# A one-core decoder step: paired attention scores, the first norm's scale and shift on VectorE, merged rows kept on chip

## The chip, the cores and the metric

The kernel runs on one core of a Trainium2 chip. The metric is the device time of one call in microseconds (us), lower is better, as the median of several runs. The core's engines are named as the profile names them: PE is TensorE (PEld its weight loads, PEq its sequencer), DVE is VectorE, ACT is ScalarE, POOL is GpSimd, SP is SyncE.

## What is computed

One layer of a decoder for 1024 prompt tokens and 8 x 8 sample tokens (1088 in all), model width 1024, in float32. Attention comes in three dilation groups over 8 head slots of 64; beside it runs a gated convolution of width 3. What the change touches is, cut from the reference:

```python
# scores of one query block of 128 against its own and the previous key block
scores = jnp.einsum('brnqhc,brnkhc->brnhqk', qb, kk) * (c ** -0.5)
...
br_a = jnp.einsum('nse,ed->nsd', y_att, w_branch_attn)
br_c = jnp.einsum('nse,ed->nsd', c_b * z_conv, w_branch_conv)
merged = jax.nn.sigmoid(g_a) * br_a + jax.nn.sigmoid(g_c) * br_c
mix = jnp.einsum('nsd,de->nse', merged, w_out)
h = layer_norm(DEEPNORM_ALPHA * x + mix, ln1_g, ln1_b)
f = peer_ffn(h, peer_w_q, peer_keys_1, peer_keys_2, peer_u, peer_v)
return layer_norm(DEEPNORM_ALPHA * h + f, ln2_g, ln2_b)
```

`peer_ffn` has 8 retrieval heads. A head scores the token against two lists of 128 keys, takes the 16 best of each, then the 16 best of the pair sums, which name 16 of 16384 experts. Each expert is one row of `peer_u` (a dot product with the token, then GELU) and one row of `peer_v` (weighed by the result and added up).

## The kernel before

**Stages.** The program is a list of phases with all engines meeting between them. The tokens are two halves: EARLY (A) is the first 512 (4 tiles of 128), LATE (B) the other 576 (4 tiles of 128, and one of the 64 sample tokens). In order, with the time at which each runs: `prompt_attn` (0 to 722 us); for A `conv_gates` (732 to 956), `branches` (to 1043) and `mix_ln1` (1045 to 1135); `retrieve_early` (to 1476); for B `conv_gates` (to 1773), `branches` (to 1873), `mix_ln1` (1874 to 2013), `retrieve` (to 2285); `build_gates` (to 2458); `experts` (2461 to 4170); `ln2_out`.

**Split products.** Nearly every product is taken in three parts: each operand is split into a high part of a shorter type (`wh`, `mh`, ACT copies it) and the rest (`wl`, `ml`, DVE or POOL subtracts), and `split3` (lines 79 to 83) issues high x high, high x low, low x high.

**Attention** (`prompt_attn`, line 87). There are 4 slot pairs `s`, each with two heads of 64, which lie in partitions 0 to 63 and 64 to 127 of `qT` and `kT`. A slot pair has 32 units: 16 of kind N (dilation 1; 8 query blocks x 2 heads) and 16 of kind R (the other two groups; 8 tiles x 2 heads). The units of the two heads of one block follow each other. For a unit, PE takes the scores against one or two key blocks per group (`scores`, line 525, into PSUM banks that rotate by three), VectorE adds the mask and takes the maximum, ScalarE takes the exponential, PE transposes the probabilities (`turn_probs`, line 535) and multiplies them with the values (`weigh_values`, line 548). Scores are issued two units ahead; the first two are issued among the last two projection tiles of the slot pair, and ScalarE takes their exponentials among its copies there (`exp`).

**Branches and mixing.** `branches` (line 908) makes the two branch products for each of 8 blocks of 128 output columns, `merge` (line 1002) multiplies them with the gates, adds them, and SyncE stores the block to `s_merged` in DRAM. SyncE loads the branch weights (`r_raw`) block by block, the first one at the start of the phase. `mix_ln1` (line 1103) reads the merged rows back, one tile of 128 tokens at a time (`m_raw`), loads the eight 512 KB blocks of `w_out` over 3 buffers (A) or 2 (B), and multiplies. `Norm` (line 1050) does the first layer norm of each tile: `stats` sums with the residual and takes mean and variance on VectorE, `root` takes the square root on ScalarE, `scale` subtracts the mean and divides on VectorE, and `affine` (lines 1097 and 1099) multiplies with `ln1_g` and adds `ln1_b` on GpSimd, which then stores the row tile to `s_h`. PE transposes the normed tile, and ScalarE and VectorE split it.

**Rows of the experts.** Half A's experts are taken row by row: for each of 512 (token tile, slot) steps GpSimd gathers a 512 KB tile of `peer_u` and one of `peer_v` (`fetch_rows`, lines 605 and 611, over a ring of 4 buffers), and VectorE does `dot_row` (line 623) and `weigh_row` (line 640). `row_step` does one step; there are 528 with the tail. The steps are laid into the phases of half B: `ROWS_IN = (60, 16, 16)` says how many lie in `conv_gates`, `branches` and `mix_ln1` of B, and the rest is in `experts`. Half B's experts are computed in `experts` for all 16384 experts with PE.

**Early retrieval** (`retrieve_early`, line 1282) does 8 retrieval heads for half A and, woven into them, the cached attention of 8 sample batches. One round of its loop takes query and key scores of one head (PE), `mask_scores` of one batch and `rank`, `pairs`, `finish` of earlier heads (VectorE), `choose` (ScalarE) and `look_up` (GpSimd), which find the index of a chosen expert by a one-hot product. SyncE's loop is

```python
for i in range(HEADS):
    if i + 1 < HEADS:
        for x in range(2):
            load_w(i + 1, x)
    load_values(i)            # waits for the value product of batch i - 1
    if i + 1 < DB:
        load_new(i + 1)       # waits for the turn of batch i
        load_keys(i + 1)
```

where `new` (line 1371) are the queries and keys of the sample tokens, which PE turns at line 1689, `KT` the cached keys and `V` (`cache_v`, line 1383) the cached values, 2.3 MB a batch.

## Time and profile before

| | |
|---|---|
| runs of the kernel | 4220.33, 4224.22, 4226.38 us; median 4224.22 |
| the profiled execution | 4224.69 us; span of its profile 4222.9 us |
| PE busy | 3685.5 us (87%) |
| DVE busy | 3001.5 us (71%) |
| ACT busy | 1240.1 us (29%) |
| POOL busy | 1843.2 us (44%) |
| DMA | 1024.51 MB, mean 243 GB/s |

The span is the time from the first to the last instruction that the profiler saw; all times of the trace are from its start. A busy time is the sum over an engine's instructions, so an engine that is at 87% over the whole span can be full in one stage and half idle in another. The slices of the span show that, each digit being tenths:

```profile
PE   8999998997676399776773999999999999999998
...
DVE  4434433333355668668687979999998999999996
...
PEclk9999998998777699988876999999999999999999
DMA  4122121896444278786201889999999999999996
```

### The profile page before, as it was taken

To read this page: it belongs to the slowest core of one execution; us is meant where nothing else is said; L and a number is where in the kernel's file an instruction comes from. 1 tells how busy PE (TensorE), PEld (TensorE's weight loads), DVE (VectorE), ACT (ScalarE), POOL (GpSimd) and SP (SyncE) were. 2 spreads that over 40 slices of the span, in tenths; PEclk is the share of its full clock that TensorE was granted. 3 is DMA by queue.
4 is the path that set the end of the run, shared out by engine and by line. 5 is a ranking of instruction groups with operands and counts; after the bars stand their busy time and mean duration, and the time that the engine had idled before them with its cause. 6 is when DMAs were issued, how large, how long until landed. Compare 5 with 4: busy or idle time off the path is not lost. (4 is left out here: it accounts for less than half of the span.)

```text
span 4222.9 us, 64289 instructions
## 1 busy us (share of the span) xinstructions
PE 3685.5 (87%) x24855; PEld 3441.4 (81%) x24855; DVE 3001.5 (71%) x5899; ACT 1240.1 (29%) x2036; POOL 1843.2 (44%) x1382
## 2 busy tenths in 40 slices
PE   8999998997676399776773999999999999999998
PEld 8899896885555299764762889999999999999996
DVE  4434433333355668668687979999998999999996
ACT  2323313221233322211334952222222222222221
POOL 0000000000334435436576956666666666666661
PEclk9999998998777699988876999999999999999999
DMA  4122121896444278786201889999999999999996
GB/s 144 26 74 68 28 74 31 329 360 200 159 145 162 73 257 311 289 308 208 75 21 34 231 289 368 371 377 375 379 381 357 376 378 378 369 364 377 378 361 220
DMA packets 485059, 1024.51 MB, mean 243 GB/s; under 512 B 50977, under 2 KB 257441, under 8 KB 482841
## 3 DMA queue, kind: packets, MB, share of 16 engines
q0 software_dynamic: 149264, 543.49, 34.5%
q1 hardware_dynamic: 334264, 472.56, 32.5%
q8 instruction: 191, 3.13, 0.3%
q10 hardware_dynamic: 1232, 4.46, 0.3%
q14 instruction: 108, 0.88, 0.1%
HBM read 942.84 MB, written 131.28 MB: 254 GB/s over the span
## 5 line engine op out<-in xcount | busy, mean ns | idle before, releaser
L605 POOL DMA_INDIRECT u_row<-in_peer_u_dram,eid x512 | 731.6, 1429 | 646.0 <-DVE dots L623 556.5
L611 POOL DMA_INDIRECT v_row<-in_peer_v_dram,eid x512 | 583.5, 1140 | 193.4 <-issue 155.8
L640 DVE SCALAR_TENSOR_TENSOR f_row<-v_row,g_coef,f_row 128x1024 f32<-128x1024 f32 x508 | 661.4, 1302 | 1.5 <-DMA v_row<-in_peer_v_dram,eid 1.2
L81 PE MATMUL e_ps<-coef_h,v_h 128*128 128x288 f32 x2048 | 614.4, 300 | 44.9 <-DVE v_l L2318 28.2
L623 DVE CUSTOM_DVE_ANT_0 u_row<-u_row,h_row 128x1024 f32<-128x1024 f32 x512 | 630.9, 1233 | 5.0 <-DMA h_row<-s_h 2.7
L81 PE MATMUL e_ps<-tokens_Bh,u_h 128*128 128x288 f32 x2048 | 608.1, 297 | 7.0 <-DVE u_l L2312 7.0
L83 PE MATMUL e_ps<-coef_h,v_l 128*128 128x288 f32 x2048 | 609.8, 298 | 0.0
L82 PE MATMUL e_ps<-coef_l,v_h 128*128 128x288 f32 x2048 | 609.2, 297 | 0.0
L82 PE MATMUL e_ps<-tokens_Bl,u_h 128*128 128x288 f32 x2048 | 607.4, 297 | 0.0
L83 PE MATMUL e_ps<-tokens_Bh,u_l 128*128 128x288 f32 x2048 | 604.6, 295 | 0.0
L81 PEld LDWEIGHTS e_ps<-coef_h,v_h 128*128 128x128 f32 x2048 | 390.2, 191 | 57.1 <-DVE v_l L2318 36.3
L81 PEld LDWEIGHTS e_ps<-tokens_Bh,u_h 128*128 128x128 f32 x2048 | 386.2, 189 | 7.5 <-DVE u_l L2312 7.5
L82 PEld LDWEIGHTS e_ps<-coef_l,v_h 128*128 128x128 f32 x2048 | 390.2, 191 | 0.0
L83 PEld LDWEIGHTS e_ps<-coef_h,v_l 128*128 128x128 f32 x2048 | 389.8, 190 | 0.0
L83 PEld LDWEIGHTS e_ps<-tokens_Bh,u_l 128*128 128x128 f32 x2048 | 387.1, 189 | 0.0
L82 PEld LDWEIGHTS e_ps<-tokens_Bl,u_h 128*128 128x128 f32 x2048 | 386.4, 189 | 0.0
L276 POOL DMA_DIRECT2D s_att<-attS x4 | 2.3, 584 | 721.7 <-ACT attS L336 721.7
L2271 ACT ACTIVATE v_h<-v_raw 128x512 fp32r<-128x512 f32 x256 | 158.8, 627 | 423.4 <-PE e_ps L83 393.3
L2256 ACT ACTIVATE x_tmp<-e_ps 128x576 f32<-128x576 f32 x128 | 83.3, 651 | 489.2 <-PE e_ps L83 488.4
L81 PE MATMUL c_psB<-tokens_Bh,c_whB 128*128 128x288 f32 x640 | 193.0, 302 | 20.5 <-DVE c_wlB L818 20.5
L82 PE MATMUL c_psB<-tokens_Bl,c_whB 128*128 128x288 f32 x640 | 191.6, 299 | 0.0
L83 PE MATMUL c_psB<-tokens_Bh,c_wlB 128*128 128x288 f32 x640 | 190.8, 298 | 0.0
(425 smaller groups left out, 8538.7 us busy)
## 6 DMA issues: line engine op xcount, KB each, us to landing
u_raw<-in_peer_uT_dram SPq DMA_DIRECT2D x128, 512.0 KB, 7.5
v_raw<-in_peer_vQ_dram SPq DMA_DIRECT2D x256, 256.0 KB, 6.6
s_g<-gate_block SPq DMA_DIRECT2D x9, 4096.0 KB, 16.3
x_gate<-s_g SPq DMA_DIRECT2D x64, 576.0 KB, 7.3
out_o_kv_sample_dram<-in_cache_kv_w_dram SPq DMA_DIRECT2D x32, 1016.0 KB, 8.0
c_rawA<-in_conv_tiles_dram SPq DMA_DIRECT2D x40, 512.0 KB, 5.6
c_rawB<-in_conv_tiles_dram SPq DMA_DIRECT2D x40, 512.0 KB, 6.3
w_raw<-in_w_in_dram SPq DMA_DIRECT2D x96, 192.0 KB, 3.7
```

The costliest lines, as they stand in the source:

```text
L81: pe.matmul(out, lh, rh, start=first, stop=False)
L82: pe.matmul(out, lh, rl, start=False, stop=False)
L83: return pe.matmul(out, ll, rh, start=False, stop=last)
L276: pool.dma_start(io["s_att"][s][:, :SEQ], attS[:]).then_inc(att_out, 16)
L605: pool.indirect_dma_start(k["u_row"][:, r % RING], None, io["peer_u"][0], bass.IndirectOffsetOnAxis(ap=k["eid"][:, r:r + 1], axis=0)).then ...
L611: pool.indirect_dma_start(k["v_row"][:, v % RING], None, io["peer_v"][0], bass.IndirectOffsetOnAxis(ap=k["eid"][:, v:v + 1], axis=0)).then ...
L623: dve.tensor_tensor_reduce(row, row, k["h_row"][:, t % 2], 1.0, 0.0, ALU.mult, ALU.add, k["dots"][:, s % 2, x:x + 1]).then_inc(k["dotted"], 1)
L640: dve.scalar_tensor_tensor(out=f, in0=row, scalar=coef, in1=f, op0=ALU.mult, op1=ALU.add).then_inc(k["weighed"], 1)
L2256: act.activation(tmp[:, e % 2].rearrange("p (y n) -> p y n", y=2), ps[:, 2 * (e % 2):2 * (e % 2) + 2, :CW], ACT.Gelu).then_inc(gelu_done, 1)
L2271: act.activation(vh[:, n % VS], vraw[:, n % VR], ACT.Copy).then_inc(v_hi, 1)
```

## The change

1. **Scores of two heads in one call.** `scores(s, u)` now issues both heads of a block, units `u` and `u + 1`: block by block of 128 keys, first partitions 0 to 63, then 64 to 127, into two PSUM banks. A pair is issued after `turn_probs(s, u)` of every even `u`; the first pair is issued at the last projection tile, and ScalarE takes its two exponentials before the copy of that tile.
2. **Branch weights.** The first block of branch weights is loaded in the middle of `conv_gates`.
3. **Merged rows stay in SBUF** (`merged_A`, `merged_B`, each in two parts), the store to `s_merged` and the loads back are gone, and the splits read the two parts. The eight blocks of `w_out` are loaded during `branches` into a place of their own.
4. **The norm.** `stats` adds a pass (y - mean) x gain on VectorE after the variance; `scale` is (y / std) + bias. `affine` is gone, and GpSimd only stores.
5. **Expert rows.** `ROWS_IN` is (60, 16, 0): the 16 steps of `mix_ln1` are done in `experts`.
6. **Early retrieval.** SyncE loads `new` and the keys of the next batch ahead of the values of this one. ScalarE's `choose` is two functions, `weights` and `one_hot`, issued at the head's start and between the queries; GpSimd's `look_up` is split in the same way into `distances` and `look_up`.

The diff, cut (unchanged in meaning where left out: the placement of the buffers in SBUF):

```diff
-ROWS_IN = (60, 16, 16)
+ROWS_IN = (60, 16, 0)
...
-                        if ri == 2 and t >= PT - 2:
-                            exp(s, t - (PT - 2))
+                        if ri == 2 and t == PT - 1:
+                            exp(s, 0)
+                            exp(s, 1)
...
             def scores(s, u):
-                kind, where, h = units[u]
...
+                kind, where, _ = units[u]
+                for x in (u, u + 1):
+                    if x >= SR:
+                        pe.wait_ge(s_free, s * NU + x - SR + 1)
...
-                off = 0
-                for g in ((0,) if kind == "N" else (1, 2)):
-                    tiles = [j for gg, j in key_blocks(u) if gg == g]
-                    n = len(tiles) * P
-                    m = pe.matmul(ps[:, s_bank(s, u), off:off + n], qT[h * HD:(h + 1) * HD, g, q * P:(q + 1) * P],
-                                  kT[h * HD:(h + 1) * HD, g, tiles[0] * P:tiles[0] * P + n], start=True, stop=True)
-                    off += n
-                m.then_inc(s_ready, 1)
+                blocks = key_blocks(u)
+                for x, (g, j) in enumerate(blocks):
+                    for h in range(2):
+                        rows = slice(h * HD, (h + 1) * HD)
+                        m = pe.matmul(ps[:, s_bank(s, u + h), x * P:(x + 1) * P], qT[rows, g, q * P:(q + 1) * P],
+                                      kT[rows, g, j * P:(j + 1) * P], start=True, stop=True)
+                        if x == len(blocks) - 1:
+                            m.then_inc(s_ready, 1)
...
-                scores(s, 3)
                 for u in range(2, NU):
-                    if u + 2 < NU:
-                        scores(s, u + 2)
...
                     turn_probs(s, u)
+                    if u % 2 == 0 and u + 2 < NU:
+                        scores(s, u + 2)
...
+                if n == NQ // 2:
+                    load_branch(sp, k, io, 0)
...
-                sp.wait_ge(br_done, NC * (j + 1))
-                sp.dma_start(io["s_merged"][j][:, cols], mg[:, j % 2]).then_inc(mg_out[j % 2], 16)
-            for x in range(2):
-                sp.wait_ge(mg_out[x], 16 * KD // 2)
+                sp.dma_start(k["w_out"][half.name][:, j], io["w_out"][0, j * P:(j + 1) * P]).then_inc(k["o_in"][j], 16)
...
         dve.bn_aggr(self.mv[:n, x], self.st[:n, x]).then_inc(self.var_ready, 1)
+        dve.drain()
+        dve.scalar_tensor_tensor(out=y, in0=y, scalar=self.mv[:n, x, 0:1], in1=self.gain[:n], op0=ALU.subtract, op1=ALU.mult)
...
-        dve.tensor_scalar(self.y[:n, x], self.y[:n, x], self.mv[:n, x, 0:1], self.rstd[:n, x:x + 1],
-                          ALU.subtract, ALU.mult).then_inc(self.scaled, 1)
-
-    def affine(self, pool, t, x, n):
-        pool.wait_ge(self.scaled, t + 1)
-        pool.tensor_tensor(self.y[:n, x], self.y[:n, x], self.gain[:n], ALU.mult).then_inc(self.gained, 1)
-        pool.wait_ge(self.gained, t + 1)
-        pool.tensor_tensor(self.y[:n, x], self.y[:n, x], self.bias[:n], ALU.add).then_inc(self.ready, 1)
-
+        dve.scalar_tensor_tensor(out=self.y[:n, x], in0=self.y[:n, x], scalar=self.rstd[:n, x:x + 1], in1=self.bias[:n],
+                                 op0=ALU.mult, op1=ALU.add).then_inc(self.ready, 1)
...
-    at_row = spread(y0, rows, [1] * (TL - 1) + [0])
+    at_row = spread(y0, rows, [1] * TL)
...
-                act.activation(mh[:, x, :, :n], raw[:, x, :, :n], ACT.Copy).then_inc(m_hi, 1)
+                for part in range(2):
+                    m = act.activation(mh[:, x, part * KD // 2:(part + 1) * KD // 2, :n], merged(i, part), ACT.Copy)
+                m.then_inc(m_hi, 1)
...
-                load_values(i)
                 if i + 1 < DB:
                     load_new(i + 1)
                     load_keys(i + 1)
+                load_values(i)
...
+                if i >= 2:
+                    weights(i - 2)
+                    one_hot(i - 2, 0)
                 if i < HEADS:
                     query(i, 0)
                     split_w(i + 1, 0)
                 if i >= 1:
                     copy_probs(i - 1)
+                if i >= 2:
+                    one_hot(i - 2, 1)
...
-                if i >= 2:
-                    choose(i - 2)
...
             for i in range(HEADS + 1):
-                if i < HEADS:
-                    for x in range(2):
+                if i >= 2:
+                    distances(i - 2)
+                for x in range(2):
+                    if i < HEADS:
                         query(i, x)
                         split_w(i + 1, x)
-                if i >= 2:
-                    look_up(i - 2)
+                    if i >= 2:
+                        look_up(i - 2, x)
```

PE in prompt attention, where the first slot pair goes over into its units of kind N, before (`a_ps` is PSUM, `S` the probabilities, `PTs` their transposes, `vR` the values; x2 is two such instructions in a row):

```order
L525 MATMUL a_ps<-kT,qT 128x256 x2
L535 MATMUL a_ps<-ident,S 128x128 x2
L548 MATMUL a_ps<-vR,PTs 128x64
L525 MATMUL a_ps<-kT,qT 128x256
L535 MATMUL a_ps<-ident,S 128x128 x2
L548 MATMUL a_ps<-vR,PTs 128x64 x2
```

and the same place in the changed kernel:

```order
L528 MATMUL a_ps<-kT,qT 128x128 x4
L551 MATMUL a_ps<-vR,PTs 128x64
L538 MATMUL a_ps<-ident,S 128x128 x2
L551 MATMUL a_ps<-vR,PTs 128x64 x2
L538 MATMUL a_ps<-ident,S 128x128 x2
L528 MATMUL a_ps<-kT,qT 128x128 x4
```

A score product of 256 columns for one head stood ahead of each unit; now four products of 128 columns, two for each head, stand ahead of every second one, between the transposes and the values of a unit.

SP in the early retrieval, one round, before (`q_rawA` are the query weights of the next head):

```order
L1382 DMA new<-s_qkv 24x1x512
L1383 DMA cache_v<-in_cache_vS_dram 128x4608
L1371 DMA new<-s_qkv 24x1x512 x2
L1376 DMA KT<-in_cache_kT_dram 128x4x128
L1377 DMA KT<-in_cache_kT_dram 128x4x1024
L1365 DMA q_rawA<-in_peer_w_q_dram 128x8x128 x2
```

and in the changed kernel:

```order
L1365 DMA q_rawA<-in_peer_w_q_dram 128x8x128 x2
L1371 DMA new<-s_qkv 24x1x512 x2
L1376 DMA KT<-in_cache_kT_dram 128x4x128
L1377 DMA KT<-in_cache_kT_dram 128x4x1024
L1382 DMA new<-s_qkv 24x1x512
L1383 DMA cache_v<-in_cache_vS_dram 128x4608
```

`new` x2 and the two loads of `KT` now stand ahead of the batch's value loads (L1382, L1383) and not behind them.

DVE in `mix_ln1` of half A, one tile, before:

```order
L1076 SCALAR_TENSOR_TENSOR n1A_y<-n1A_res,m_psA 128x1024
L1080 BN_STATS n1A_st<-n1A_y 128x6 x2
L1082 BN_AGGR n1A_mv<-n1A_st 128x2
L1090 RECIPROCAL n1A_rstd<-n1A_std 128x1
L1092 TENSOR_SCALAR n1A_y<-n1A_y,n1A_mv,n1A_rstd 128x1024
```

and in the changed kernel:

```order
L1084 SCALAR_TENSOR_TENSOR n1A_y<-n1A_res,m_psA 128x1024
L1088 BN_STATS n1A_st<-n1A_y 128x6 x2
L1090 BN_AGGR n1A_mv<-n1A_st 128x2
L1092 SCALAR_TENSOR_TENSOR n1A_y<-n1A_y,n1A_mv,n_affineA 128x1024
L1100 RECIPROCAL n1A_rstd<-n1A_std 128x1
L1102 SCALAR_TENSOR_TENSOR n1A_y<-n1A_y,n1A_rstd,n_affineA 128x1024
```

The pass with the gain stands between the variance and the root's result, and the last pass adds the bias.

## Rows read from the trace of the kernel before

**Rows 1.** Windows: stretch, length, busy us of each engine, PEclk, DMA share, GB/s.

```profile
0.00:732.00 732.00, 699.50 (x4232) 641.02 (x4232) 290.81 (x795) 211.95 (x576) 2.54 (x8) 0.99 0.22 62
...
300.00:370.00 70.00, 69.76 (x438) 57.50 (x437) 30.98 (x118) 35.99 (x110) 0.00 (x0) 1.00 0.13 28
...
1140.00:1476.00 336.00, 201.76 (x1754) 161.00 (x1754) 185.80 (x956) 109.76 (x194) 146.46 (x80) 0.73 0.41 142
...
1886.00:2016.00 130.00, 76.52 (x282) 54.69 (x282) 93.00 (x101) 23.53 (x28) 72.66 (x48) 0.75 0.62 209
...
2460.00:4173.00 1713.00, 1660.37 (x12288) 1647.74 (x12288) 1578.72 (x2100) 451.10 (x694) 1094.13 (x848) 0.99 0.97 365
```

**Rows 2.** Timeline of TensorE in attention: start, us, line, operation, shapes, [idle before].

```profile
318.81 0.70 PE L525 MATMUL a_ps<-kT,qT 64*128 64x256 f32 x2
319.44 0.44 PE L535 MATMUL a_ps<-ident,S 128*128 128x128 f32 x2
...
320.20 0.70 PE L525 MATMUL a_ps<-kT,qT 64*128 64x256 f32 x2
...
328.52 0.71 PE L525 MATMUL a_ps<-kT,qT 64*128 64x128 f32 x4
```

**Rows 3.** Timeline of TensorE in the early retrieval: transposes, and 32-column strips.

```profile
1213.56 1.14 PE L1713 MATMUL q_psA<-ident,Ss 128*128 128x128 f32 x9
...
1222.75 2.17 PE L1725 MATMUL q_psA<-cache_v,PTss 128*32 128x128 f32 x72
```

**Rows 4.** Timeline of ScalarE: the first branch weights, early and late.

```profile
968.66 1.48 ACT L985 ACTIVATE r_whA<-r_rawA 128x1536 fp32r<-128x1536 f32 x1 [12.86 <-DMA r_rawA<-in_w_branch_conv_dram]
...
1778.17 1.48 ACT L985 ACTIVATE r_whB<-r_rawB 128x1536 fp32r<-128x1536 f32 x1 [11.43 <-DMA r_rawB<-in_w_branch_conv_dram]
```

**Rows 5.** Timeline of the mixing stages, early, then late (from 1874.52).

```profile
1041.79 0.69 DVE L1012 TENSOR_TENSOR r_mgA<-r_mgA,r_tcA 128x512 f32<-128x512 f32 x1
...
1053.14 0.77 PE L81 MATMUL m_psA<-o_whA,m_hA 128*128 128x512 f32 x1 [12.85 <-DVE o_wlA L1213]
...
1081.02 1.22 DVE L1076 SCALAR_TENSOR_TENSOR n1A_y<-n1A_res,m_psA 128x1024 f32<-128x1024 f32 x1 [7.58 <-PE m_psA L83]
...
1108.71 1.21 DVE L1076 SCALAR_TENSOR_TENSOR n1A_y<-n1A_res,m_psA 128x1024 f32<-128x1024 f32 x1
...
1121.36 1.21 DVE L1076 SCALAR_TENSOR_TENSOR n1A_y<-n1A_res,m_psA 128x1024 f32<-128x1024 f32 x1
...
1125.73 2.33 POOL L1097 TENSOR_TENSOR n1A_y<-n1A_y,n1A_gain 128x1024 f32<-128x1024 f32 x1 [6.88 <-DVE n1A_y L1092]
...
1874.52 0.06 DVE L1072 MEMSET n1B_eps<- 128x1 f32 x1 [0.42 <-PEq L912]
...
1920.06 1.22 DVE L1076 SCALAR_TENSOR_TENSOR n1B_y<-n1B_res,m_psB 128x1024 f32<-128x1024 f32 x1 [8.15 <-PE m_psB L83]
...
1925.42 3.41 DVE L640 SCALAR_TENSOR_TENSOR f_row<-v_row,g_coef,f_row 128x1024 f32<-128x1024 f32 x1
...
1940.42 1.21 DVE L1076 SCALAR_TENSOR_TENSOR n1B_y<-n1B_res,m_psB 128x1024 f32<-128x1024 f32 x1
```

**Rows 6.** Waits, 1135 to 1476: engine, line, waited for: us, times, longest.

```profile
PE q_psA L1689 <- DMA new<-s_qkv: 72.1, 7, 12.4
```

**Rows 7.** Timeline of VectorE in the early retrieval, one head.

```profile
1179.37 1.38 DVE L1633 CUSTOM_DVE_ANT_0 Ss<-q_psA,smask 128x1176 f32<-128x1176 f32 x1 [7.28 <-PE q_psA L1702]
...
1217.15 1.38 DVE L1633 CUSTOM_DVE_ANT_0 Ss<-q_psA,smask 128x1176 f32<-128x1176 f32 x1 [7.82 <-PE q_psA L1702]
...
1224.24 3.75 DVE L1583 TENSOR_TENSOR candA<-top_vA 128x256 f32<-128x256 f32 x2
...
1237.02 0.23 DVE L1604 TENSOR_TENSOR pos_parts_fA<-best_pos_fA,row_firstA 128x64 f32<-128x64 f32 x1
...
1255.96 0.68 DVE L1618 TENSOR_REDUCE selA<-q_hotA 128x64 f32<-128x512 f32 x1 [9.08 <-issue]
```

**Rows 8.** Windows: a stretch in the middle of the expert stage.

```profile
3300.00:3500.00 200.00, 197.67 (x1485) 196.80 (x1485) 190.04 (x253) 54.52 (x83) 134.66 (x105) 1.00 0.99 379
```

170 lines of the change are left out of this document (91 added, 79 removed).

## The prediction

> **What bounds the kernel now.** I read the busy time by stage first. The reader is to see five different limits [rows 1]. In prompt attention (0 to 732 us) TensorE is busy 699.5 of 732. In the early retrieval (1140 to 1476) it is busy 201.8 of 336 at a mean granted clock of 0.73, with the DMA engines at 0.41, so something waits there. In the late mixing stage (1886 to 2016) it is busy 76.5 of 130. In the expert stage (2460 to 4173) TensorE is at 1660 of 1713, VectorE at 1579 and the DMA engines at 0.97: three resources are nearly full. The stages follow each other behind barriers, so a gain in one is a gain at the end, if a later stage isn't given more work. This change does both.
>
> **Paired scores.** Attention handles 32 units for each of 4 slot pairs. A unit's score product of 256 columns is two passes that hold TensorE 0.63 us (318.81 to 319.44) of a unit of 1.39 us (to 320.20) [rows 2]. A unit with two products of 128 columns takes four passes in 0.71. One pair has 14 units of the first kind, 2 of half that, 8 with four short passes, and 8 with two 256-column products: 14 x 0.63 + 2 x 0.32 + 8 x 0.64 + 8 x 1.26 = 24.7 us, 98.6 for all four. The change issues the same columns as passes of 128, alternating between partitions 0 to 63 and 64 to 127. If the two halves of the array work at once, this halves: -49 us. No row shows two row halves at work together. The nearest shows four column strips: 72 passes of 128 columns in 2.17 us, 0.03 each, against 1.14 for 9 passes across the whole array, 0.13 each [rows 3]. So work in separate parts of the array does overlap here, by four. What is late next: ScalarE is busy 36.0 us over 32 units, 1.12 each (300 to 370 us) [rows 1], and TensorE would need 1.39 - 0.31 = 1.08 for a two-block unit. ScalarE, or the chain score, mask, exponential, transpose, which now has less work of TensorE to hide under, takes some back in the first 16 units. I give it 4 us: **-45**. The ends: 0 (no overlap; the columns are the same) and -55 (switching between array shapes half as often).
>
> The Trainium skill (TensorEngine Tiling, Tiling Modes and Theoretical Speedup) says that two tiles of 64 rows run in parallel, up to 2 times as fast. By it alone this term is -49; no row here shows it for row tiles.
>
> **Weights of the branches loaded ahead.** ScalarE waited 12.9 us (early) and 11.4 (late) for the first branch weights [rows 4]; 8.1 and 4.7 of it lie behind the stage's start, since loads were only issued there. They now land during the convolution stage. The attention rows that the branches also need still load at the start, so I take 6 early; late, where 4 MB of output weights come into a stage that also gathers expert rows, 2.5. **-8.5**. The ends: 0 and -13. The 0.8 MB added to each convolution stage I put at **+1** together.
>
> **Merged rows kept on chip, output weights loaded ahead.** Early: the first output matmul starts at 1053.14, 10.7 us after the last merge, and the first tile is summed at 1081.02 [rows 5]. Between them TensorE waits for eight 512 KB weight loads over two or three buffers. Now nothing is stored and read back, and all eight lie in SBUF. What remains ahead of the first matmul is two splits (some 1.3 us each on ScalarE and VectorE) and the first weight split, another pass of 1.2: some 4.3 us with the starts. The eight splits go at VectorE's 1.23 us, so the first half tile takes 10.4, about its pace at the low clock, and the second 24 matmuls x 0.23 = 5.6: 16 us for 28. That is -6.4 - 11.4 = -17.8. Late: the sum at 1920.06 is 45.5 us after the stage's start at 1874.52 [rows 5]; in its place stand 4.1 and 16.4: -25.
>
> **The norm and the sixteen rows.** GpSimd's two passes stood between VectorE and the transposes: 2.33 each early, 4.7 and a start together, and not less late [rows 5]. VectorE now does (y - mean) x gain in one pass of about 1.25 beside ScalarE's root, and one more in place of the scale. The wait behind a tile falls by 3.5 to 4 us. It counts at the last tile of each half, with 0.6 to 1 at the one before. Between them tiles are paced by TensorE at 12.65 us (1108.71 to 1121.36), where VectorE needs some 8 us. -5 early, -4 late. Late, tiles take 20.4 us (1920.06 to 1940.42), because four row steps of VectorE lie in each and are caught by GpSimd: a weighing step that ends beside it takes 3.41 us. With 16 rows gone and GpSimd quiet they should take the early 12.7 to 13: 4 x -7.2 = -29. Sum of this and the part before: -22.8 early, -58 late, **-81**. Ends: -60, -92.
>
> **Early retrieval.** TensorE waits 72.1 us in seven waits for `new` [rows 6]. SyncE issues it only after `load_values`, which waits for the previous batch's value product; and its 0.1 MB then stand in the queue behind 2.3 MB of values. The change issues `new` and the keys a whole head earlier, so the wait should go. What is late next is VectorE: mask, one rank and the pairs run without a gap from 1217.15 to 1237.25 (20.1 us); the other rank takes what this one did, 5.7 from the mask's end to 1224.24, and the two parts of `finish` some 2.2 [rows 7]. That is 28.0 us a head, with starts 28.2, where a head took 37.8 (mask to mask, 1179.37 to 1217.15) and TensorE's busy time is 201.8 over 8 heads. `finish` waited 9.08 us for the look-up [rows 7]. Moving the one-hot work to the start of a head on ScalarE and GpSimd puts it beside mask, rank and pairs, and I cost the moved instructions at nothing under that cover of some 20 us; uncovered they would be 10 to 15 a head. Seven heads x 9.5: **-66**. Ends: -45, -72.
>
> **Experts.** The 16 rows come here. Each is two gathers of 512 KB, in all 16.8 MB, and 16 x 2.5 us of VectorE, which would be busy 1619. The stretch 3300 to 3500 shows the DMA engines at 0.99 with 379 GB/s [rows 8]. At this rate 16.8 MB are 44 us of all engines. There is slack of some 10 to 15 us in the middle of the stage (shares of 0.98 to 0.99) and none that these rows can reach at its ends. **+35**. Ends: +5 and +50.
>
> The Trainium skill (DMA: Bandwidth & Descriptors, Where 436 GB/s comes from) puts the ceiling at 435 GB/s. By it 379 is not full, the rows would fit, and the sum below would be 30 us lower. The same page's HBM limit of 358 is already exceeded by the row.
>
> **The sum:** -45 - 8.5 + 1 - 81 - 66 + 35 = -164.5. The profiled execution took 4224.69 us (span 4222.9); that gives 4060. It is 0.5 above the median, so the forecast is **4060** against 4224.22. A difference of 0.2% (8.4 us) is about what a measurement can tell.
>
> **Rivals.**
> - *The halves don't overlap.* Two row halves write the same PSUM partitions, which column strips do not. Attention then gains nothing: 4060 + 45 = 4105. The strips speak against it. 8%.
> - *The expert stage takes the rows for nothing.* For: VectorE waits for gathered rows almost nowhere, GpSimd waits for VectorE. Against: the share of 0.99. Then 4060 - 30 = 4030. 10%.
> - *The retrieval finds another wait.* In SyncE's new order the value load of one batch stands ahead of the next head's query weights; if these come late, or ScalarE, which now waits for VectorE at the head's start, delays the next query's copy, a head takes 32 and not 28: -40 for -66, so 4086. 12%.
> - *The change doesn't do what it says:* the loads ahead land late and the mixing stages keep half of their waits: 4060 + 25 = 4085. 4%.
> - *Slower: starved experts lose the clock.* The granted clock is 1.00 in the stretch shown and 0.73 where TensorE waits [rows 1, 8]. A 288-column matmul comes every 0.135 us (1485 in 200) and would come every 0.27 at the low level. If gathers delay weights so that TensorE idles often, 1270 of 12288 matmuls at the low level give back 172 us, the 164 and 0.2%. That is a mean clock of 0.95 for 0.99 in the stage. The stage would have to be starved ten times as much as its present loss. Time from 4233 on. 2%.
>
> **How the numbers follow.** My forecast has 64%, its own range 4040 to 4085. To hold 8 in 10 I add the case of no overlap and that of free rows, and leave out the far ends: **4028 to 4100**. Faster than before by over 0.2% is all but the last rival and a little for what I don't see: 0.97; within 0.2% 0.01; slower 0.02.
>
> **What would show it.** In the profile after: attention ends near 675 instead of 722, with score pairs of 0.6 to 0.7 us (1.26 if the halves don't overlap). The wait of TensorE for `new` is gone, and a head lasts 27 to 29 us. No wait for output weights in the mixing stages, tiles of 12.5 to 13 us in both. The expert stage lasts some 1748 us with the DMA engines at 0.98 or more, TensorE's busy share down to about 0.95 and new waits for `v_raw` and `u_raw` or for gathered rows. If the stage still lasts 1713, my reading of the DMA share is wrong; if a head still takes over 32, my reading of the retrieval is.

## The result, and the profile after

The changed kernel takes 4022.68 us (median of 4 runs, 4021.18 to 4025.86) against 4222.62 for the kernel before in the same comparison: a ratio of 0.9527, 95% interval 0.9510 to 0.9543. The forecast was 4060 with a range of 4028 to 4100, so the sign was right and the time lay 5 us below the range. The profiled execution took 4025.86 us, with a span of 4024.1 for 4222.9 before: -198.8 where the sum said -164.5. Among all the executions behind this document one stands apart: of the four of run e11 one took 12239.65 us at a granted clock of 0.41, the others 4012 to 4016; e11's median below counts it, its ratio doesn't.

Each stage's length below is read in the two timelines, from the first instruction of a phase to the first of the next one, with the forecast's term beside it.

| stage | before | after | change | forecast |
|---|---|---|---|---|
| attention | 727.0 | 691.0 | -36.0 | -45 |
| convolution, early | 232.5 | 231.8 | -0.7 | +0.5 |
| branches, early | 84.8 | 78.3 | -6.5 | -6 |
| mixing, early | 90.1 | 66.9 | -23.2 | -22.8 |
| early retrieval | 341.2 | 259.1 | -82.1 | -66 |
| convolution, late | 297.1 | 297.1 | 0.0 | +0.5 |
| branches, late | 101.1 | 95.8 | -5.3 | -2.5 |
| mixing, late | 138.6 | 77.5 | -61.1 | -58 |
| retrieval, late | 273.2 | 268.0 | -5.2 | 0 |
| gates of the experts | 172.6 | 172.6 | 0.0 | 0 |
| experts | 1711.5 | 1733.0 | +21.5 | +35 |
| last norm | 52.5 | 52.3 | -0.2 | 0 |

The windows of the changed kernel, with the columns of [rows 1], show the same five stages:

```profile
0.00:692.00 692.00, 659.15 (x4472) 621.84 (x4472) 285.40 (x795) 206.53 (x576) 2.55 (x8) 0.99 0.23 64
...
1069.00:1328.00 259.00, 188.11 (x1754) 147.26 (x1754) 194.85 (x960) 111.27 (x194) 147.46 (x81) 0.82 0.54 187
...
1720.00:1798.00 78.00, 63.39 (x280) 48.72 (x280) 47.04 (x60) 19.93 (x29) 4.68 (x8) 0.89 0.28 100
1798.00:2066.00 268.00, 146.19 (x1010) 142.85 (x1010) 208.25 (x1109) 94.63 (x155) 172.47 (x97) 0.76 0.11 32
...
2239.00:3972.00 1733.00, 1668.86 (x12288) 1658.10 (x12288) 1615.98 (x2150) 451.11 (x697) 1132.13 (x880) 0.98 0.98 370
```

In the early retrieval TensorE has the same 1754 matmuls in 259 us and not 336, at a granted clock of 0.82 for 0.73. In the late mixing stage GpSimd is busy 4.7 us where it was busy 72.7. The expert stage moves 370 GB/s for 365 at a DMA share of 0.98 for 0.97. The late retrieval, in which nothing was changed, gained 5.2 us; its granted clock is 0.76 (0.74 before), and TensorE's busy time there is 6.3 us shorter for the same matmuls.

**Attention.** TensorE's timeline of the changed kernel, in the first units of a slot pair:

```profile
302.67 0.71 PE L528 MATMUL a_ps<-kT,qT 64*128 64x128 f32 x8
303.32 0.43 PE L551 MATMUL a_ps<-vR,PTs 128*128 128x64 f32 x2
...
304.92 0.71 PE L528 MATMUL a_ps<-kT,qT 64*128 64x128 f32 x8
...
307.64 0.44 PE L538 MATMUL a_ps<-ident,S 128*128 128x128 f32 x2 [0.81 <-ACT S L317]
308.01 0.71 PE L528 MATMUL a_ps<-kT,qT 64*128 64x128 f32 x8
```

Eight passes of 128 columns hold TensorE 0.65 us (302.67 to 303.32), where four took 0.64 [rows 2]. So the two halves of the array do work at once. Sixteen passes (a pair with two key blocks in each of two groups) hold it 1.09 us, where eight passes of 256 columns for the same two units took 2 x 1.06 before. The grouped lines say it for the whole stage, before (two groups) and after:

```profile
L525 PE MATMUL a_ps<-kT,qT 64*128 64x256 f32 x240 | 72.3, 414 | 0.0
...
L525 PE MATMUL a_ps<-kT,qT 64*128 64x128 f32 x144 | 26.6, 300 | 0.0
```

```profile
L528 PE MATMUL a_ps<-kT,qT 64*128 64x128 f32 x624 | 52.0, 293 | 0.0
```

The scores take 52.0 us for 98.9, a gain of 46.9, and the stage gained 36.0. The other 11 are given back at several places. Most pairs of eight passes follow each other by 2.24 us where two units took 2 x 1.39 = 2.78, so 0.54 of the 0.61 is kept. One of the first pairs takes 3.09 (304.92 to 308.01), with a wait of 0.81 for ScalarE's exponential; nine such waits in the stage add up to 4.7 us. And the first pair of sixteen passes is followed by the next one after 3.38 us, where its two units took 2 x 1.82 before.

**Early retrieval.** No wait for `new` is left among TensorE's waits. VectorE's timeline, two heads in a row:

```profile
1161.78 1.38 DVE L1643 CUSTOM_DVE_ANT_0 Ss<-q_psA,smask 128x1176 f32<-128x1176 f32 x1 [0.23 <-PE q_psA L1712]
...
1168.87 3.79 DVE L1593 TENSOR_TENSOR candA<-top_vA 128x256 f32<-128x256 f32 x2
1172.58 2.38 DVE L1597 CAST top_ifA<-top_iA 128x128 f32<-128x128 uint32 x1
...
1189.97 1.38 DVE L1643 CUSTOM_DVE_ANT_0 Ss<-q_psA,smask 128x1176 f32<-128x1176 f32 x1
...
1197.41 0.69 DVE L1593 TENSOR_TENSOR candA<-top_vA 128x256 f32<-128x256 f32 x2
1198.02 0.22 DVE L1597 CAST top_ifA<-top_iA 128x128 f32<-128x128 uint32 x1
```

The first of these two heads lasts 28.19 us, the forecast's 28.2 to the tenth. But the pair sums and the cast, 6.2 us in it, take 0.9 in the next head. That one lasts 25.4 and not 23, since two of its later passes are slow in their place (1.42 and 1.19 us, for 0.23 and 0.26 in the first). What stands beside the slow pair sums and cast is in GpSimd's timeline:

```profile
1168.66 1.28 POOL L1527 TENSOR_TENSOR q_lA<-q_fullA,q_hA 128x512 fp32r<-128x512 f32 x1
1169.90 2.54 POOL L1523 TENSOR_TENSOR q_wlA<-q_rawA,q_whA 128x1024 fp32r<-128x1024 f32 x1
1172.40 2.48 POOL L1540 TENSOR_TENSOR q_hotA<-q_hotA,top_ifA 128x1024 f32<-128x1024 f32 x1
```

VectorE's passes end at 1172.66 and 1174.96; GpSimd's end at 1172.44 and 1174.88. Each VectorE pass is done 0.1 to 0.2 us after a GpSimd pass ends. The seven heads, from mask to mask, take 22.5, 23.9, 25.0, 28.2, 25.4, 28.4 and 26.1 us, 25.6 on average. Before they took 24.4, 37.8, 46.0, 38.6, 36.8, 38.7 and 37.6, 37.1 on average. The 46.0 is the head from 1217.15 to 1263.14 [rows 7]:

```profile
1246.11 0.22 DVE L1609 TENSOR_REDUCE totA<-exA 128x4 f32<-128x64 f32 x1 [8.86 <-ACT exA L1434]
...
1263.14 1.38 DVE L1633 CUSTOM_DVE_ANT_0 Ss<-q_psA,smask 128x1176 f32<-128x1176 f32 x1
```

The first two heads have less to do than the others: in the loop the pair sums start with the second head and `finish` with the third.

**Mixing.** The first output product and the first two tile sums of the late stage, which starts at 1720.76:

```profile
1724.46 0.77 PE L81 MATMUL m_psB<-o_whB,m_hB 128*128 128x512 f32 x1 [10.23 <-DVE o_wlB L1213]
...
1738.96 1.22 DVE L1084 SCALAR_TENSOR_TENSOR n1B_y<-n1B_res,m_psB 128x1024 f32<-128x1024 f32 x1 [5.49 <-issue]
...
1753.12 1.21 DVE L1084 SCALAR_TENSOR_TENSOR n1B_y<-n1B_res,m_psB 128x1024 f32<-128x1024 f32 x1
1756.09 1.28 DVE L1092 SCALAR_TENSOR_TENSOR n1B_y<-n1B_y,n1B_mv,n_affineB 128x1024 f32<-128x1024 f32 x1
1757.52 1.28 DVE L1102 SCALAR_TENSOR_TENSOR n1B_y<-n1B_y,n1B_rstd,n_affineB 128x1024 f32<-128x1024 f32 x1
...
1765.09 1.21 DVE L1084 SCALAR_TENSOR_TENSOR n1B_y<-n1B_res,m_psB 128x1024 f32<-128x1024 f32 x1
```

The first product comes 3.7 us after the start (forecast 4.1), the first sum 18.2 after it (forecast 20.5; 45.5 in [rows 5]). The first two sums are 14.2 us apart, the others 12.0 (forecast 12.5 to 13) for 20.4.

### The profile page after: what moved, and what is told of

Same layout as the page of the kernel before. It is cut to its first block and busy times, and to the rows that moved or that the text cites. A ratio compares the mean times of both kernels' runs of the same rounds, so it can differ in the third digit from the quotient of the medians.

```text
span 4024.1 us, 64681 instructions
## 1 busy us (share of the span) xinstructions
PE 3616.4 (90%) x25095; PEld 3404.7 (85%) x25095; DVE 2998.9 (75%) x5917; ACT 1229.7 (31%) x2041; POOL 1790.2 (44%) x1364
## 5 line engine op out<-in xcount | busy, mean ns | idle before, releaser
L642 DVE SCALAR_TENSOR_TENSOR f_row<-v_row,g_coef,f_row 128x1024 f32<-128x1024 f32 x508 | 652.7, 1285 | 3.9 <-DMA v_row<-in_peer_v_dram,eid 2.8
L625 DVE CUSTOM_DVE_ANT_0 u_row<-u_row,h_row 128x1024 f32<-128x1024 f32 x512 | 621.8, 1215 | 5.1 <-DMA h_row<-s_h 2.8
L2266 ACT ACTIVATE x_tmp<-e_ps 128x576 f32<-128x576 f32 x128 | 83.2, 650 | 419.7 <-PE e_ps L83 400.7
L81 PE MATMUL c_psB<-tokens_Bh,c_whB 128*128 128x288 f32 x640 | 192.6, 301 | 20.5 <-DVE c_wlB L834 20.5
## 6 DMA issues: line engine op xcount, KB each, us to landing
s_g<-gate_block SPq DMA_DIRECT2D x9, 4096.0 KB, 16.1
```

What stands on the lines that cost most here:

```text
L81: pe.matmul(out, lh, rh, start=first, stop=False)
L625: dve.tensor_tensor_reduce(row, row, k["h_row"][:, t % 2], 1.0, 0.0, ALU.mult, ALU.add, k["dots"][:, s % 2, x:x + 1]).then_inc(k["dotted"], 1)
L642: dve.scalar_tensor_tensor(out=f, in0=row, scalar=coef, in1=f, op0=ALU.mult, op1=ALU.add).then_inc(k["weighed"], 1)
L2266: act.activation(tmp[:, e % 2].rearrange("p (y n) -> p y n", y=2), ps[:, 2 * (e % 2):2 * (e % 2) + 2, :CW], ACT.Gelu).then_inc(gelu_done, 1)
```

## The experiments

All are the changed kernel with one edit, unless said otherwise. "The call" is the median; ratios are to the kernel before, run in the same comparison. The early retrieval, where it wasn't edited, lasted from 249.8 to 259.1 us over twelve profiles (mean 254.3), so 5 us in that stage of one profile tell nothing; the changed kernel's own profile has the longest of them, and by the other eleven this stage gained more than 82 us. Attention, where it wasn't edited, lasted 688.5 to 691.0, the early branch stage 75.2 to 79.0, the late one 95.1 to 97.0. The interval of a ratio is about 7 us to either side. Stages are read in one profile a run, with the marks of the table above; the expectations of e1 to e4 take attention, the early retrieval and late mixing by other marks (680.9, 256.6 and 81 us where the table has 691.0, 259.1 and 77.5).

### Do the halves of the array need to alternate? (e1, e7)

```diff
-                for x, (g, j) in enumerate(blocks):
-                    for h in range(2):
+                for h in range(2):
+                    for x, (g, j) in enumerate(blocks):
```

> The changed kernel, with the four (or eight) passes of a score pair issued head by head: all passes of partitions 0 to 63 first, then all of 64 to 127. Same passes, same place. In the changed kernel attention lasts 680.9 us (716.7 before) and eight passes of 128 columns take 0.71 us. If it is the alternation that lets the two halves of the array work at once, eight passes take some 1.1 to 1.3 us again and attention some 700 to 725 us, the call some 4045 to 4065. If TensorE overlaps the halves in whatever order they come, or if the gain is that a pair switches the array's shape half as often, attention stays at 681 and the call at 4023.

4023.31 us, 0.9525 (0.9509 to 0.9540), the same as the changed kernel within the interval. But attention lasted 696.6 us, outside the 688.5 to 691.0 of the others, and the rows say why. The pairs of eight passes hold TensorE 0.65 us as before, those of sixteen 1.64 and not 1.09. Here is e1, then the changed kernel, then one unit of the two before:

```profile
303.60 0.72 PE L528 MATMUL a_ps<-kT,qT 64*128 64x128 f32 x8
...
167.82 1.71 PE L528 MATMUL a_ps<-kT,qT 64*128 64x128 f32 x16
```

```profile
168.05 1.16 PE L528 MATMUL a_ps<-kT,qT 64*128 64x128 f32 x16
```

```profile
347.88 1.13 PE L525 MATMUL a_ps<-kT,qT 64*128 64x256 f32 x4
```

All four such pairs of every slot pair are like this, 16 x 0.55 = 8.8 us, and the scores take 61.1 us in all for 52.0. So with four passes of one half in a row the order doesn't matter; with eight in a row about half of the overlap is lost (2 x 1.06 = 2.12 without any, 347.88 to 348.94 being one unit). Why it is lost there is not shown. The first rival of the expectation is thus right for the long pairs and wrong for the short ones.

> The changed kernel, with the scores of a pair issued as before the change in passes of up to 256 columns, the one head's behind the other's. If it is enough that work of both halves of the array stands next to each other in TensorE's queue, attention stays at 691 us (679 to 695) and the call at 4023, perhaps a little less since half as many passes and weight loads are issued. If the short passes matter for the overlap, score pairs of two key blocks take some 1.26 us and not 0.65, and attention lasts 715 or more.

The edit puts the old loop over groups of up to 256 columns inside a loop over the two heads. 4019.19 us, 0.9516 (0.9500 to 0.9531); attention 689.2 us. A pair of two key blocks is four passes in 0.63 us, and the long pair is eight passes, four for each head in a row, in 1.07. So short passes aren't needed, and it is the number of passes in a row that cost e1 its overlap, not their columns, which are the same here. Whether this is faster than the changed kernel isn't shown (the intervals overlap).

### What the two new orders of the early retrieval are worth (e2, e3, e6)

```diff
+                load_values(i)
                 if i + 1 < DB:
                     load_new(i + 1)
                     load_keys(i + 1)
-                load_values(i)
```

> The changed kernel, with SyncE's old order in the early retrieval: the values of a batch ahead of the next batch's new rows and keys. The stage lasts 256.6 us in the changed kernel, 338.6 before. If the wait for the new rows was what set the pace, the stage comes back to 320 to 338 us and the call to 4085 to 4105, with TensorE waiting some 60 to 72 us for new rows. If the moved one-hot work was as much of it, the stage stays below 310.

4093.73 us, 0.9691 (0.9675 to 0.9707): 71 us given back. The stage lasts 329.0 us, its heads behind the first 37.4 to 37.7, and the wait is there again among TensorE's waits:

```profile
PE q_psA L1699 <- DMA new<-s_qkv: 69.2, 7, 11.5
```

> The changed kernel, with the look-up of ScalarE and GpSimd back at the end of a head, and SyncE's new order kept. If the look-up only hides under VectorE, the stage stays within 5 us of 256.6. If VectorE's last step of a head waits for it once the new rows are early, the 9 us wait is there again and the stage lasts some 290 to 320 us (10 to 15 us a head uncovered, part of it under what SyncE gained), the call 4055 to 4085.

The edit puts `weights` and both `one_hot` calls behind `keep(i - 1)`, and `distances` and both `look_up` calls behind the loop over `x`, as they stood before. 4046.16 us, 0.9581 (0.9565 to 0.9597): 23 us. The stage lasts 280.4, less than expected, its third head 36.1 and the later ones 29.8 to 30.4. So SyncE's order alone brings 341.2 to 280.4 (-60.8), the look-up's place alone 341.2 to 329.0 (-12.2), and both together -82 to -91. Of the 12.2 the third head has 8.5 (46.0 to 37.5): in it VectorE has its slow passes beside GpSimd and then waits 8.86 us for ScalarE and 9.08 for the look-up [rows 7], and the next mask stands right behind. In the four heads after it the look-up's place brings 0.4 us each while TensorE waits for `new`, and some 3 once it doesn't.

```diff
                 dve.tensor_tensor_reduce(S[:], flat[:, S0:S0 + W], mask[:], SCALE, LOW, ALU.add, ALU.max, mx[:])
                 dve.drain()
+                dve.tensor_tensor_reduce(S[:], flat[:, S0:S0 + W], mask[:], SCALE, LOW, ALU.add, ALU.max, mx[:])
+                dve.drain()
```

> The changed kernel, with VectorE's mask pass of the early retrieval (1.38 us, once a batch) issued twice, which gives the same result and 1.5 us more of VectorE in each of 8 heads. The stage lasts 259 us. If VectorE sets the pace of the heads now, +10 to 12 us. If TensorE's own products or ScalarE's copies do, 0 to 4 us.

4035.01 us, 0.9545 (0.9530 to 0.9561): 12.3 more, and 270.0 us in the stage, 15.7 above its mean. Eight passes of 1.5 are 12. VectorE sets the pace of the heads behind the first.

### What a VectorE pass waits for beside GpSimd (e11, e18)

In e11 GpSimd's passes of 1024 elements in the early retrieval are two of 512, one after the other; here the look-up's, the other two likewise:

```diff
-                pool.tensor_tensor(hot[:, x], hot[:, x], ixf[:, h % 2, x].unsqueeze(2).to_broadcast([P, TL, K, K]),
-                                   ALU.mult)
+                for a in (slice(0, TL // 2), slice(TL // 2, TL)):
+                    pool.tensor_tensor(hot[:, x, a], hot[:, x, a],
+                                       ixf[:, h % 2, x, a].unsqueeze(2).to_broadcast([P, TL // 2, K, K]), ALU.mult)
```

> The changed kernel, with GpSimd's passes of 2.4 us in the early retrieval (weight splits, distances, look-up) issued as two halves each. Heads there take 23.9 to 28.8 us, and in the long ones VectorE's pair sums take 3.8 us and not 0.8. If such a pass of VectorE waits until GpSimd's running pass ends, its slow passes shrink to 1.2 to 1.5 us, and the stage falls by 5 to 12 us below 253 to 259. If the two share a path at a lower rate, or VectorE waits until GpSimd has nothing left, the pair sums stay at 3.8 in the heads that meet GpSimd and the stage is the same within 3 us.

4014.32 us (4012.57 over the other three), 0.9499 (0.9480 to 0.9518), an interval that overlaps the changed kernel's. The stage lasted 247.2 us, its heads after the first two 25.1 to 25.8 where they had been 25 or 28. VectorE's cast beside GpSimd's passes of this kernel:

```profile
1190.57 1.30 DVE L1602 CAST top_ifA<-top_iA 128x128 f32<-128x128 uint32 x1
```

```profile
1188.96 1.48 POOL L1529 TENSOR_TENSOR q_lA<-q_fullA,q_hA 128x512 fp32r<-128x512 f32 x1
1190.39 2.61 POOL L1524 TENSOR_TENSOR q_wlA<-q_rawA,q_whA 128x512 fp32r<-128x512 f32 x2
```

The cast ends at 1191.87, not with the pair of GpSimd's passes (1193.0) but about where its first half ends (1190.39 + 2.61 / 2 = 1191.7). A slow cast is 1.3 us now and was 2.4, a slow pair sum 1.4 and was 2.5: VectorE's pass waits until the running pass of GpSimd ends. The Trainium skill says so (SBUF — State Buffer, Who interferes with whom): the two engines have one port pair in common, which a GpSimd instruction that reads SBUF holds to its end, while a VectorE instruction with two SBUF inputs, or a copy or cast in a two-port mode, waits. These rows agree for the pair sums and the cast. With e15 and e16, which have the same halves (251.1 and 248.0 us), the stage is 248.8 us on average of three profiles, for 254.3.

> The changed kernel, with GpSimd's passes of 2.4 us in the early retrieval in quarters. With halves VectorE's slow passes fell from 2.5 to 1.4 us and the call to 4014.3 (0.9499 of before). If VectorE waits for the end of the running pass, they fall to 0.8 to 1.0, and the stage by 2 to 4 us more, unless what a further start costs GpSimd makes the look-up late: then the stage grows by 3 or more, and VectorE waits for it again.

4017.24 us, 0.9514 (0.9495 to 0.9532), the stage 252.7: no further gain, against the expected 2 to 4 us. Some slow passes did fall to 0.75 us, but the longest stayed at 1.3 to 1.5, since GpSimd's passes of 1.3 us (the query's split, the look-up's fold) were not cut. GpSimd's weight splits now take 45.4 us in all and not 38.5.

### The late mixing stage (e9, e10, e12, e4, e13)

e9 restores `tensor_scalar` in `scale`, `affine` on GpSimd and its two semaphores, and takes the pass with the gain out of `stats`.

> The changed kernel, with the norm's scale and shift back on GpSimd (two passes of 2.33 us a tile behind VectorE), no expert rows in the mixing stages. The mixing stages last 66.9 (early) and 77.5 us (late). If the passes only count at the end of a half and a little before, as forecast, +5 early and +4 late, the call +9. If GpSimd's passes slow VectorE's splits and sums in every tile, +2 or more a tile, the call +18 or more. If they are hidden, 0.

4028.78 us, 0.9531 (0.9515 to 0.9547). The stages last 72.2 (+5.3) and 83.9 (+6.4), where 5 and 4 were forecast. 3.4 us of each lie behind the last sum (13.7 and 12.6 us to the stage's end, for 10.3 and 9.2), the other 1.9 and 3.0 between the sums.

e10 takes the load of `w_out` out of the loop of `branches`, and in `mix_ln1` it reads

```diff
+            for j in range(KD):
+                sp.dma_start(k["w_out"][half.name][:, j], io["w_out"][0, j * P:(j + 1) * P]).then_inc(k["o_in"][j], 16)
             N.load(sp)
```

> The changed kernel, with the eight loads of the output weights at the start of the mixing stage in place of the branch stage, into the same eight buffers, the merged rows kept on chip. 4 MB take 11 to 12 us, and the first product waits for the first block and the norm's loads. Mixing stages +8 to +12 each (the rest of the 23 and 61 us came from the buffers, the norm and the rows), branch stages -1 to -5 each since they load 4 MB less. If the early loads are hidden in the branch stage for nothing, those stay at 78 and 96.

4030.67 us, 0.9535 (0.9519 to 0.9551). Mixing 72.2 (+5.3) and 85.7 (+8.2); branches 75.2 (-3.1) and 95.1 (-0.7), no shorter than in other runs that keep the loads there. So the early loads cost the branch stages nothing that these profiles can tell, and the early mixing stage gave back less than the 8 expected.

> The changed kernel, with the 16 expert rows back in the late mixing stage, spread over its five tiles. The expert stage lasts 1732.7 us in the changed kernel and 1711.2 before. It should come back to 1711, which gives the price of 16 rows there, 21 us and not the 35 forecast. In the mixing stage (81 us now) the rows cost 16 x 2.5 = 40 us of VectorE in tiles of 12.7 us where VectorE needs 8: if GpSimd's two passes were what made them dear, +20 to 25 us and the call the same as the changed kernel within 5 us; if the rows themselves are dear beside the norm, +30 to 40 and the call 10 to 20 us slower.

4028.35 us, 0.9533 (0.9518 to 0.9549), with `ROWS_IN = (60, 16, 16)`. Experts 1711.1 (-21.9), mixing 93.7 (+16.2). The 16 rows cost there less than the 20 to 25 expected. But the late retrieval lasted 285.3 (+17.3). TensorE's waits in it name a small table:

```profile
PE q_psB L2021 <- DMA count16B<-in_c_count_dram: 15.7, 1, 15.7
```

> The changed kernel, with 16 expert rows back in the late mixing stage, over its first four tiles only. With five tiles the late retrieval lasted 285.3 us for 268.0, and TensorE waited 15.8 us for its small count table. If that wait came from the gathers issued behind the last tile, the retrieval is back at 268, the mixing stage stays at 94 to 98 and the expert stage at 1711, and the call takes 4016 to 4021. If not, the retrieval stays at 285 and the call at 4028.

Beside `ROWS_IN`, e12 has

```diff
-    at_row = spread(y0, rows, [1] * TL)
+    at_row = spread(y0, rows, [1] * (TL - 1) + [0])
```

4026.46 us, 0.9529 (0.9513 to 0.9545). The table's wait is 5.0 us as in the changed kernel; the retrieval lasts 276.2, mixing 95.8 (+18.3), experts 1710.7. So the gathers behind the last tile caused the long wait, though the retrieval didn't come all the way back to 268. e4's profile is of the slowest of its four executions (4034.61), and the medians of e4 and e12 are 1.9 us apart: whether the others had the long wait isn't shown. Rows in the mixing stage are no better than rows with the experts.

The late retrieval's length differs with the number of row steps done ahead of it, but neither grows nor falls with it: 273.2 to 276.2 us with 92 (the kernel before, e8, e12, e13), 266.2 to 268.3 with 76 (the changed kernel and every one with its rows), 271.5 with 60 (e5). In e8 none of the 92 lay in the mixing stage, so gathers still under way are not the reason. What is stays open.

e13 is e9 and e12 together.

> The changed kernel, with both the norm's scale and shift back on GpSimd and 16 expert rows in the first four tiles of the late mixing stage. Alone the first cost that stage 6.4 us (83.9 for 77.5) and the second 18.3 (95.8). If they add up, the stage lasts 102. If rows and GpSimd's passes lengthen each other, as the kernel before suggests with tiles of 20.4 us, it lasts 110 to 125, and a weighing step beside GpSimd takes 3.4 us again.

4044.96 us, 0.9573 (0.9557 to 0.9589). The late mixing stage lasts 111.8 us, 34.3 more than in the changed kernel, of which 6.4 and 18.3 are the two alone and 9.6 their meeting. One tile of it, VectorE:

```profile
1756.26 1.21 DVE L1084 SCALAR_TENSOR_TENSOR n1B_y<-n1B_res,m_psB 128x1024 f32<-128x1024 f32 x1
...
1761.61 3.41 DVE L642 SCALAR_TENSOR_TENSOR f_row<-v_row,g_coef,f_row 128x1024 f32<-128x1024 f32 x1
1768.29 1.27 DVE L642 SCALAR_TENSOR_TENSOR f_row<-v_row,g_coef,f_row 128x1024 f32<-128x1024 f32 x1
...
1776.61 1.20 DVE L1084 SCALAR_TENSOR_TENSOR n1B_y<-n1B_res,m_psB 128x1024 f32<-128x1024 f32 x1
```

and GpSimd's pass beside it:

```profile
1760.63 3.30 POOL L1105 TENSOR_TENSOR n1B_y<-n1B_y,n_affineB 128x1024 f32<-128x1024 f32 x1 [0.89 <-issue]
```

The tile is 20.35 us and the first weighing step 3.41, as in [rows 5]. It ends at 1765.02, 1.1 us behind GpSimd's pass, which is about its own time when alone; GpSimd's pass in its turn takes 3.30 us for 2.33. The rest, 138.6 - 111.8 = 26.8 us, is by subtraction the merged rows and output weights. e10 gave back 8.2 for the time of loading, which would leave some 19 for the round trip through DRAM and the two buffers; no run put these back.

### The price of a row (e5, e8)

> The changed kernel, with the 16 expert rows of the late branch stage moved to the expert stage as well (60, 0, 0). 16 rows cost the expert stage 21.5 us when they came from the mixing stage (1711.5 to 1733.0) where 44 were expected of full DMA engines. If the stage had slack which the first 16 rows partly filled, the next 16 cost 35 to 44 and the stage lasts 1768 to 1777 us. If the price is a steady 1.35 us a row, whatever bounds the stage, it lasts some 1755. The late branch stage (95.8 us) loses 16 rows and should fall by some 10 to 20.

`ROWS_IN = (60, 0, 0)`: 4041.26 us, 0.9569 (0.9553 to 0.9585). Experts 1757.2 (+24.2), late branches 83.2 (-12.6), in a profile of the fastest of its four executions (4032.64). The expert stage of e4 (16 rows fewer than the changed kernel) and of e5 (16 more), as windows:

```profile
2269.00:3980.00 1711.00, 1656.81 (x12288) 1643.61 (x12288) 1578.92 (x2098) 450.90 (x694) 1099.51 (x848) 0.99 0.97 365
```

```profile
2221.00:3978.00 1757.00, 1675.06 (x12288) 1666.87 (x12288) 1652.23 (x2198) 450.75 (x698) 1175.02 (x912) 0.97 0.99 375
```

The DMA engines' share goes from 0.97 over 0.98 to 0.99, the rate from 365 over 370 to 375 GB/s. Two digits are too few for the idle time; summed over the packets of the three traces it is 47, 40 and 26 us. So the first 16 rows, 44 us of transfers at 379 GB/s, took 6 us from the idle time and made the stage 22 longer, and the next took 14 and made it 24 longer. The other 16 and 6 us are no idle time at all: the transfers as a whole got faster, 2.66, 2.64 and 2.63 us of all engines per MB. The middle of the stage shows it, without its first 91 and last 90 us. Before, changed and e5:

```profile
2550.00:4080.00 1530.00, 1493.95 (x11093) 1482.46 (x11092) 1436.46 (x1921) 401.84 (x622) 1013.91 (x787) 0.99 0.99 375
```

```profile
2330.00:3882.00 1552.00, 1501.97 (x11085) 1492.51 (x11084) 1470.95 (x1966) 401.43 (x623) 1048.05 (x817) 0.98 0.99 379
```

```profile
2312.00:3888.00 1576.00, 1511.91 (x11121) 1504.89 (x11121) 1507.31 (x2016) 402.38 (x627) 1089.18 (x849) 0.97 1.00 383
```

At a share of 0.99 the engines still took more bytes a us. Why is not shown. TensorE's busy time grows as well, by 12 and 6.

> The changed kernel, with 16 rows more in the late convolution stage and 16 fewer in the expert stage (76, 16, 0). There VectorE is busy 217 of 297 us and the DMA engines at 0.79. If the expert stage's rows cost 1.35 us each, it falls by 21.5 to 1711. If the convolution stage hides rows under its products, it grows by 0 to 6 and the call takes 4002 to 4010. If its 16.8 MB have to wait for its own weights' loads, it grows by 15 to 25 and the call stays at 4020 to 4026.

`ROWS_IN = (76, 16, 0)`: 4024.93 us, 0.9523 (0.9505 to 0.9541), no change. Experts 1714.6 (-18.4), late convolution 313.4 (+16.3), with the DMA share there 0.89 for 0.79.

### What attention gave back (e14, e17), and what adds up (e15, e16)

e14 issues ScalarE's eight splits of the next weights in units 4, 5, 6, 7, 9, 11, 13, 15 in place of 1, 3, ... 15.

> The changed kernel, with ScalarE's first four splits of the next slot pair's weights issued in units 4 to 7 of attention, in place of units 1, 3, 5 and 7. In the first three slot pairs the fourth score pair comes 3.10 us after the third, in the last one, where no such splits are issued, 2.75, and later ones 2.24. If ScalarE's splits are what holds up the first units, attention falls by 1 to 3 us (0.35 to 1 in each of three slot pairs). If the chain score, mask, exponential, transpose alone does it, nothing changes beyond 0.5 us, or the splits hold up the units 4 to 7 in their place.

4017.62 us, 0.9517 (0.9501 to 0.9533), attention 690.7 us for 691.0, and not the 1 to 3 less that were expected if the splits hold up the first units. The fourth pair comes after 2.75 us and not 3.10, but three of the next pairs take 2.34 or 2.35 and not 2.24. The splits hold up whichever unit they stand in.

```diff
-                    turn_probs(s, u)
                     if u % 2 == 0 and u + 2 < NU:
                         scores(s, u + 2)
+                    turn_probs(s, u)
```

> The changed kernel, with each score pair issued before the even unit's transposes in place of behind them. The chain score, mask, exponential, transpose then starts some 0.4 us earlier. If this chain is what takes back 9 us of the 45, the first pairs of a slot (3.38 and 3.10 us) shorten by 0.3 to 0.5 and attention by 2 to 4 us, below 688. If the pairs are held by TensorE's own work and the free score banks, attention stays at 689 to 691.

4012.53 us, 0.9501 (0.9484 to 0.9519). Attention lasts 684.0 us, 7.0 less:

```profile
300.66 0.71 PE L528 MATMUL a_ps<-kT,qT 64*128 64x128 f32 x8
...
302.86 0.71 PE L528 MATMUL a_ps<-kT,qT 64*128 64x128 f32 x8
...
305.26 0.71 PE L528 MATMUL a_ps<-kT,qT 64*128 64x128 f32 x8 [0.19 <-DVE stat L417]
...
307.88 0.71 PE L528 MATMUL a_ps<-kT,qT 64*128 64x128 f32 x8
```

The pairs are 2.20, 2.40 and 2.62 us apart, for 2.24, 3.10 and 2.24, and later ones 2.15. A wait for `stat` (VectorE's maximum) has come to stand before the scores, a short one. No wait for ScalarE's exponential is left among TensorE's waits. Of the 1.9 us that a slot pair gains from its first to its last scores, 0.8 lie at the first pair of sixteen passes (2.59 us for 3.38), some 0.6 in the steady pairs and the rest in the first ones. So the chain behind the scores was what was late, and scores issued 0.4 us earlier feed it better. The steady pairs are now closer than the 2 x 1.12 us that the prediction had for ScalarE.

> The changed kernel, with GpSimd's passes in the early retrieval in halves and the score pairs in passes of up to 256 columns. Alone the first took the call from 4022.7 to 4014.3 and the second to 4019.2. If both are real and add, 4008 to 4012; if the second was noise, 4013 to 4016.

4013.93 us, 0.9497 (0.9482 to 0.9513): e11's time and no less, and attention is 690.4 us. No gain of e7's edit is to be seen.

> The kernel of the run before with the later weight splits of ScalarE too. If the splits were what held up the first units, 1 to 3 us less than that one; if not, the same within 1.5 us.

4014.81 us, 0.9500 (0.9484 to 0.9516): the same.

The fastest versions are thus e11, e15, e16 and e17, at 0.950 of the kernel before, not to be told apart. They are some 0.3% below the changed kernel, with intervals that overlap its own; the 7 us of e17 in attention stand clear of the 688.5 to 691.0 of the others. The half passes and the early scores lie in different stages; no run has both.

## Why the prediction was wrong, by its steps

- **Scores, -45: -36.** The overlap of the halves was right: the scores take 52.0 us for 98.9, -46.9 where half was -49. The alternation that the change relies on matters for the long pairs alone (e1). One reading of the term was off: a unit of two 256-column products holds TensorE 1.06 us and not 1.26. What failed is the 4 us for ScalarE and its chain: 11 were given back. I took them from ScalarE's mean load (1.12 us a unit against 1.08) and for the first 16 units alone. e17 shows it to be mostly a matter of order: with the pair issued behind a unit's transposes the chain starts late, in the units of kind R too, and 7 of the 11 come back when it is issued ahead of them. The rival of no overlap fell at once.
- **Branch weights, -8.5: -11.8.** Late 5.3 for 2.5. I had charged the late stage for 4 MB of output weights; by e10 they cost it 0.7 us, less than the 1.9 by which that stage differs between profiles.
- **Merged rows, weights and norm, -81: -84.3.** Right, and each part near where it was put: first product and first sum within 2.5 us, the norm's end +5.3 and +6.4 in e9, the meeting of rows and GpSimd rebuilt in e13.
- **Early retrieval, -66: -82.** The wait and its cause were right (e2), VectorE as the next bound too (e6), and a head of 28.2 us is in the trace. The step that failed is "seven heads x 9.5": one head, 37.8 us before and 28.2 after, was taken for all seven. The gains are 1.9, 13.9, 21.0, 10.4, 11.4, 10.3 and 11.5 us, 80.3 in all, and 1.8 lie outside of the heads. Against 7 x 28.2 the changed kernel's heads are 17.9 us shorter together. 10.0 of these are the first two, which lack the pair sums or `finish`. The other 7.9 are heads in which VectorE meets less of GpSimd: of the 28.2 us, 5.7 were the pair sums and the cast beside GpSimd, in their slow form, and free of it they take 0.9. Against 7 x 37.8 the heads before are 4.8 shorter together: the first was only 24.4, and the third, in which the slow passes and the waits for ScalarE and the look-up add up, was 46.0. The rows of the other heads before had all of this (the pair sums 0.42 + 0.35 and the cast 0.22 us at 1384; a head of 46.0 from the very mask at 1217.15 on which the 28.2 was built). That the moved look-up costs nothing under its cover was right, and it is worth more than nothing: 23 us by e3.
- **Experts, +35: +21.5.** The step that failed is that I took 379 GB/s at a share of 0.99 for full engines, with 44 us for the rows and 9 of them free. The middle of the stage took more at the same share (375, 379 and, at 1.00, 383 GB/s with 0, 16 and 32 more rows than before). That gave the first 16 rows 16 us and the idle time 6, and 22 were left. Each row costs 1.3 to 1.5 us and not 2.7 (44 / 16). The +22 lies between the forecast and the rival of free rows.
- **Late retrieval, 0: -5.2.** Not forecast. Its work is the same. Its length differs with the number of row steps ahead of it, by a way that the runs don't show.
- **The rates.** By the ceiling of 435 GB/s that the Trainium skill states (DMA: Bandwidth & Descriptors, Where 436 GB/s comes from) the rows would have fitted for nothing. It was right that 379 is not full, and wrong that they fit: the stage grew by 21.5 us. In the middle of e5 a share of 1.00 came with 383 GB/s, and the highest slice on its page is 395.

Against the sum, early retrieval brought 16.1 us more than its term, experts cost 13.5 less, late retrieval gave 5.2, mixing 3.5, branches 3.3 and the rest 1.9 more, and attention 9.0 less: 34.5 together, 34.3 against the rounded sum. Of the terms that had ends only the early retrieval left its own ends: -72 was the most that it was allowed, and it brought 82. That end stood on the same head as the term itself. Without these 10 us, or with +35 for the experts, the time would lie in the range, so it took both to put it outside. That attention fell short hid 9 us of them.
